# A decoder step on one core: a projection's k products split between the sample boundary and the steps inside a sample

## What is computed

```
s_s = einsum('btgrd,btgkjd->btgrkj', q, ks) * sc
p_s = masked_softmax(s_s, mask_s);  o_s = p_s @ vs
p_w = masked_softmax(einsum('btgrd,bsgd->btgrs', q, kw) * sc, mask_w);  o_w = p_w @ vw
```

```
x + gate * einsum('bte,ed->btd', y, w_out)      # D = 1024: 8 column tiles, each a sum over 8 k blocks
rmsnorm over x afterwards needs the sum of squares of all 8 tiles
```

## Time and profile before

| | |
|---|---|
| median of 3 runs | 1428.68 us (1427.25 to 1432.44) |
| the profiled execution | 1435.32 us |
| its span, first to last instruction | 1433.6 us |
| mean granted TensorE clock, as a share of full | 0.923 |
| PE, DVE, ACT, POOL busy | 89%, 33%, 29%, 10% of the span |
| the stage of the samples, first to last out tile start | 1136.67 to 1374.34 us, 237.67 us |

### The profile page before, as it was taken

The page is one execution under the profiler, slowest core; times in us unless marked ns, Lnnn a source line. Parts: engine busy times, 40 slices in busy tenths (PEclk is TensorE's granted clock), DMA queues, the critical chain, the costliest instruction groups (busy, mean ns, idle before and its releaser), DMA issues. The chain is left out here.

```text
span 1433.6 us, 25439 instructions
## 1 busy us (share of the span) xinstructions
PE 1277.2 (89%) x9335; PEld 812.4 (57%) x9335; DVE 476.5 (33%) x1463; ACT 411.1 (29%) x1083; POOL 148.0 (10%) x273
## 2 busy tenths in 40 slices
PE   4799999993877979999999899999999888888888
PEld 2576755752655744647778655555555344444448
DVE  0342120004554140202200365555555333333333
ACT  2312111112220040000101165555566243333340
POOL 0000000001000000000000122222222222222200
PEclk9899999995887989999997599999999899999985
DMA  8414333339002131113100566666667687888851
GB/s 362 176 59 176 117 117 117 117 129 291 3 25 101 59 130 59 59 59 109 50 0 1 185 232 226 223 229 226 229 231 249 237 302 290 296 297 305 297 201 67
DMA packets 77032, 238.00 MB, mean 166 GB/s; under 512 B 10987, under 2 KB 16237, under 8 KB 71405
## 3 DMA queue, kind: packets, MB, share of 16 engines
q1 hardware_dynamic: 56428, 169.26, 33.4%
q0 software_dynamic: 20480, 67.13, 12.5%
HBM read 227.68 MB, written 17.05 MB: 171 GB/s over the span
## 5 line engine op out<-in xcount | busy, mean ns | idle before, releaser
L379 PE MATMUL ps<-arena,wring 128*128 128x288 f32 x1664 | 418.1, 412 | 7.4 <-DMA wring<-in_weights 3.3
L379 PEld LDWEIGHTS ps<-arena,wring 128*128 128x128 f32 x1664 | 317.6, 192 | 99.9 <-issue 5.7
L1490 POOL DMA_DIRECT2D arena<-in_cmp_pages x128 | 69.9, 547 | 490.8 <-issue 278.7
L386 PE MATMUL ps<-wring,arena 128*128 128x512 f32 (+1 forms) x240 | 107.6, 607 | 7.1 <-ACT arena L1190 7.1
L2031 DVE CUSTOM_DVE_ANT_1 arena<-ps,small 128x512 f32<-128x512 f32 x64 | 44.4, 693 | 119.3 <-PE ps L1950 119.1
L1584 DVE CUSTOM_DVE_ANT_0 wring<-ps,wring 128x128 f32<-128x128 f32 (+3 forms) x128 | 57.7, 487 | 75.8 <-PE ps L1513 74.4
L386 PEld LDWEIGHTS ps<-wring,arena 128*128 128x128 f32 (+1 forms) x240 | 43.4, 184 | 67.3 <-issue 67.3
L1576 ACT ACTIVATE wring<-ps 128x128 f32<-128x128 f32 (+3 forms) x128 | 49.0, 436 | 90.7 <-PE ps L1536 90.7
L1562 ACT ACTIVATE wring<-wring 128x128 f32<-128x128 f32 (+3 forms) x128 | 70.7, 559 | 9.0 <-DVE wring L1584 9.0
L2018 ACT ACTIVATE arena<-ps 128x512 f32<-128x512 f32 x72 | 43.0, 597 | 103.3 <-PE ps L1971 103.3
L2007 ACT ACTIVATE arena<-arena 128x512 f32<-128x512 f32 (+1 forms) x88 | 57.0, 648 | 51.7 <-DVE arena L2047 51.7
(11 more groups left out here) (368 smaller groups left out, 1587.6 us busy)
## 6 DMA issues: line engine op xcount, KB each, us to landing
wring<-in_weights SPq DMA_DIRECT2D x27, 2048.0 KB, 8.5
arena<-in_cmp_pages SPq DMA_DIRECT2D x128, 256.0 KB, 3.5
arena<-in_cmp_pages POOLq DMA_DIRECT2D x128, 256.0 KB, 4.4
arena<-in_kv_pages SPq DMA_DIRECT2D x64, 256.0 KB, 7.4
arena<-in_kv_pages POOLq DMA_DIRECT2D x64, 256.0 KB, 6.4
wring<-in_kv_pages SPq DMA_DIRECT2D x64, 256.0 KB, 8.0
wring<-in_kv_pages POOLq DMA_DIRECT2D x64, 256.0 KB, 6.7
arena<-in_out_tiles SPq DMA_DIRECT2D x16, 512.0 KB, 6.2
```

The costliest lines, as they stand in the source:

```text
L379: last = pe.matmul(out[:, 0:HT], w[:, k, ct * P:ct * P + P], moving[k][:, half * HT:half * HT + HT], start=(k == 0), stop=(k == KT - 1))
L386: last = pe.matmul(main[0:m, :], moving[k][:, index * P:index * P + m], w[:, k, :], start=(k == 0), stop=(k == KT - 1))
L1490: eng.dma_start(cring[q % CR][:, 2 * half + j, :], v["cmp_pages"][bass.ds(ids[2 * d + j], 1)] .rearrange("o p c -> (o p) c")).then_inc(c_i ...
```

## The change

Of an out tile, the k products 0 to 3 stay at the boundary and 4 to 7 run one by one at the end of the steps 2, 4, 6 and 8. The tile is therefore done in step 8 and not at the boundary. The load of the next tile moves behind pair 3 on SP's queue, with its wait for `tile_done`. DVE's `dve_out_tile` and `dve_square` move from the boundary and item 3 to item 8 (NG), ahead of the window's `dve_scores`. The last sample (n = 7) keeps its whole tile at the boundary.

```
-        def pe_out_tile(pe, n):
-
-            pe.wait_ge(tile_in, 16 * (n + 1))
-            if n == 0:
-                pe.wait_ge(dve_a, DV3["o", 7])
-            else:
-                pe.wait_ge(tile_added, n)
-            for k in range(KT):
+        def pe_out_tile(pe, n, ks):
+
+            if ks[0] == 0:
+                pe.wait_ge(tile_in, 16 * (n + 1))
+                if n == 0:
+                    pe.wait_ge(dve_a, DV3["o", 7])
+                else:
+                    pe.wait_ge(tile_added, n)
+            for k in ks:
                 last = pe.matmul(ps[:, 0, :], tile_w[:, k, :], zT[:, k, 0:TP], start=(k == 0), stop=(k == KT - 1))
-            last.then_inc(tile_done, 1)
+            if ks[-1] == KT - 1:
+                last.then_inc(tile_done, 1)
...
                         load_kv(sp, 0, n, pair)
-                        if pair == 1:
+                        if pair == 3:
                             sp.wait_ge(*((tile_done, n) if n else (pe_c, PC_["turn", NB - 1, 1])))
                             sp.dma_start(lohi_[:, 0:1024], v["out_tiles"][n]).then_inc(tile_in, 16)
                     load_window(sp, n)
...
-                    pe_out_tile(pe, n)
+                    pe_out_tile(pe, n, range(KT // 2) if n < NB - 1 else range(KT))
...
                             pe_scores(pe, n + 1, at - 2)
+                        if n < NB - 1 and at in (2, 4, 6, 8):
+                            pe_out_tile(pe, n, [3 + at // 2])
...
-                    dve_out_tile(dve, n)
                     if n:
                         dve_out_gate(dve, n - 1)
                     for i in range(NJ):
+                        if i == (NG if n < NB - 1 else 0):
+                            dve_out_tile(dve, n)
+                            dve_square(dve, n)
                         if n < NB - 1:
                             dve_scores(dve, n + 1, i)
-                        if i == 3:
-                            dve_square(dve, n)
```

## The result

| | before | after |
|---|---|---|
| median of the runs | 1429.03 us (1427.25 to 1432.44) | 1447.23 us (1444.43 to 1448.64) |
| ratio to before, 95% interval | | 1.0122 (1.0098 to 1.0146) |
| the profiled execution | 1435.32 us | 1444.43 us |
| its span | 1433.6 us | 1442.8 us |
| seven samples, first to last whole boundary | 237.67 us | 250.09 us |

What follows compares the result with a forecast made beforehand. PE was taken to bound the boundary and DMA the sample's inside. Window at +25.0, last scores 1.31, boundary 5.9 and clock 1.3 gave 33.5 us a sample, 234 for seven, 3.7 less; median 1425 us, range 1411 to 1439.

Steps and rivals of the forecast that it cites:

- The bound: Each sample: PE bounds the boundary while DMA idles, then DMA bounds the inside while PE idles; mean 33.95 us.
- The rival that the change does not do what it says: At the boundary: DMA's idle stretch would stay as long as it is; chance 0.02.
- The boundary: Out tile's start to the end of item 0's values: 9.0 us becomes 5.9, a saving of 3.1 us.
- The step walk: From the end of item 0's values: last added product ends at +18.65, PE ready for the window at +21.2 us.
- The queue's term: SP holds the window's load for tile_done: it lands at +25.0, between +24.2 and +26; PE stands 3.8 us.
- The clock: Behind the window wait the granted clock falls, costing 1.3 us a sample, between 0 and 3.2.
- my sum of 234: Forecast for the seven-sample stretch: 234 us against 237.67, 3.7 us less.
- The edits at nothing: DVE's moved calls, covered by 2.3 us, and tile 0's earlier load, at most 1.35 us once: both taken as nothing.
- From the profile to the median: Whole kernel: profiled execution forecast at 1431.6 us, less its 6.6 us offset above the median, gives 1425.
- The slower rival: Window late, clock low over most of the boundary and first steps: 246.4 us for seven samples, median 1437; chance 0.20.
- my 33.5: Forecast length of one sample in us: 32.2 from the walk, queue and boundary, plus 1.3 for the clock.

Runs made afterwards that it cites:

- the run with work in the wait: The changed kernel with five added, unread matmuls right before the window's scores in each of seven samples: 1441.00 us, ratio to before 1.0070.

## Why the prediction was wrong, point by point

- **The bound.** Right. A sample was bound by PE at the boundary and by DMA inside, and moving the tile's matmuls out of the boundary pays: about 19 us, with the window held or not, and 28 us with nothing late behind it. The waits for groups fell from 21.5 us to none. The rival that the change does not do what it says is out. One sign that I had named did not come: DMA's idle stretch at the boundaries was to be 3 us shorter, and from the second boundary on it is 4.3 to 6.3 us where it was 4.3 to 5.5 (in slices of 0.25 us). With the window ahead of the tile it is at most 2.8, so the hold took this part of the gain.
- **The boundary, 3.1 us saved, 5.9 us left.** Right: 5.8 us at full clock.
- **The step walk.** Right within 0.3 us: the last product ends at +18.9 (predicted +18.65), PE is ready at +21.3 (+21.2), SP's issues come at +18.96 and +19.34 (+18.85 and 0.45 later), no wait for the groups 3 to 7 in the list of waits.
- **The queue's term.** This is the step that failed: the mechanism was right, the size was not. The window's scores began at +27.0 where I had +25.0 and an upper bound of +26. PE's wait was 5.6 us on average and not 3.8: 1.8 x 7 = 12.5 us, which turns the forecast gain of 3.7 us in the stretch into a loss. Counted from its own issue, I had the window landing after 5.7 us, 5.2 of them for the bytes of tile and window, and it took 7.8 in six samples. I had allowed 0.5 us for POOL's halves and took 1.35 as the most. It was the halves of groups 0 and 1, 1.05 MB, that were under way, and holding them back gives 1.5 us; the half of group 2, which I had named, costs nothing measurable. That is 1.0 of the 2.1 us. The other 1.1 is there without any other load: 6.3 us on the mean of six, and the landing differs from sample to sample by 1.7 us in that run and by 1.4 in the changed kernel, which one isolated pair of tiles could not show. Why it is longer and scatters stays open. The last sample, which has no POOL halves, landed after 5.6 us and its wait was 3.7 us, close to what I took for all seven.
- **The clock, 1.3 us a sample, between 0 and 3.2.** Inside its bounds and too small: 1.9 us a sample, by PE's busy time for the same matmuls and by the first four samples of the run with work in the wait. In the sample shown the scores and their follow-up take 2.4 us and not 1.3, and the matmuls behind them 0.5 us longer; the clock was at 0.50 from about 1271.7, 3.4 us before PE resumed, until 1278.5. In all, the stretch is 16 us above my sum of 234: 12.5 by the window, 4 by the clock, and the rest of the walk within 1 us.
- **The Trainium skill's rule** (TensorE: Matmul & The Clock Gate, "HAM oscillation — how this bites in real kernels"), that a loop whose tiles each wait for a DMA starts them cold. The trace after agrees: the granted clock fell to 0.50 with each of the seven waits of 3.7 to 6.8 us, and the stretches shown above are at 0.87 to 0.97. What I read from the trace before, that it falls for waits of 1.93 us and more, did not hold. With the window ahead of the tile it stayed at 1.00 behind waits of 2.02 and 2.04 us and fell behind one of 2.16. The tile halves behind the last two (start, us):

```profile
1197.18 3.70 PE ps L2093 x8
1287.27 5.40 PE ps L2093 x8
```

- **The edits at nothing.** DVE's move is shown to cost nothing in the kernel before.
- **From the profile to the median.** I subtracted 6.6 us because the profiled execution of before lies that far above its median. The one of after lies 2.8 us below its own. That is 9 of the 22 us between forecast and result. The other 13 are the 16 us of the stretch, less an earlier start of this stage by 4.5 us in this execution, and about 1 us that the last whole tile takes longer at the low clock (8.1 us and not 7.1). Such an offset belongs to one execution and not to a kernel; it should have widened the range.
- **The rivals.** The slower rival named this mechanism (SP held, then a long wait, then a low clock), with 1437 us and a chance of 0.20. It was what happened, though most of it by the landing and not by the clock: of the 2.2 us a sample above my 33.5, 1.8 are the longer wait and 0.6 the clock, with 0.2 saved elsewhere. Its price of 246.4 us for the stretch was 3.7 too small.

## What to carry to other kernels

A wait put into a queue that issues loads holds everything behind it in program order: before a step is moved, list what is queued behind its wait and when each of these was free to go. Here the window had been free since step 6, and letting it pass turned a loss of 1.2% into a gain of 1.3%, with the matmuls placed as they were. And when PE's wait for a late transfer is costed, the other queue's transfers already under way belong to it, and so does a low clock behind the wait.

## What the runs showed of the hardware

- Transfers issued later on the same queue did not delay an earlier one measurably (window landing 7.78 us on the mean without a hold, 8.01 with), while 1.05 MB issued before it from the other queue cost 1.5 us.
- With no other load around it, a window of 1 MB behind a tile of 0.5 MB landed 5.5 to 7.2 us after its issue. In the slowest of these 1.9 us passed after the last bytes had moved, in another 0.5.
- In the changed kernel the granted clock fell to 0.50 with each of seven PE waits: in the six of 5.4 to 6.8 us before PE resumed, in the one of 3.7 us 0.5 us after. With matmuls in the wait it fell once, where a wait of 3.2 us was left. The same matmuls kept PE busy 195.64 us at 1.00 and 208.81 us in the changed kernel.
- No one length divides the shorter waits: the clock fell behind 1.93 us and 2.16 us and stayed at 1.00 behind 2.02 and 2.04 us.
